# Moving elementwise terms of a recurrent layer from VectorE to ScalarE, one chunk later, and a longer lead into the output projection

## The chip, the cores and the metric

The program runs on one core of one Trainium2 chip. Five engines of the core matter here: TensorE (PE in the profile, its weight loads PEld), VectorE (DVE), ScalarE (ACT), GpSimd (POOL) and SyncE (SP, which issues the weight transfers). The metric is device time in microseconds of one execution. The kernel before took 3607.97 us, the median of three runs (3603.24 to 3646.27). The change is judged by the same metric; lower is better.

## What is computed

Two blocks run over one sequence of 256 tokens of width 2048. The change touches only the last layer of the second block: a recurrent layer with 4096 inner channels, followed by its output projection.

```python
def causal_depthwise_conv(x, w, b):            # w: 4 taps
    ...
    for k in range(CONV_WIDTH):
        y = y + xp[:, k:k + S] * w[k]
...
def rglru(x, wa, ba, wx, bx, lam):
    r = sigmoid(x @ wa + ba); ig = sigmoid(x @ wx + bx)   # per block of 256 channels
    log_a = -LRU_C * r * softplus(-lam)
    a = exp(log_a)
    mult = sqrt(max(-expm1(2.0 * log_a), 0.0))
    h[t] = a[t] * h[t - 1] + mult[t] * ig[t] * x[t]
...
u, z = split(rmsnorm(x) @ w_in)
y = rglru(conv(u)) * silu(z)
x = x + rmsnorm(y @ w_out)
```

The kernel writes -expm1(2 log a) as (a * a + 1) * tanh(-log a): the names below follow that ("th" the tanh, "ex" a, "q" its square, "v" the product, "mx" the max with 0, "sr" the square root).

## The kernel before, in words

**Tiles.** Activations lie transposed: channels on the 128 partitions, the 256 tokens along the row. All weights stream through in chunks of 128 x 2048 numbers (1 MB). A chunk c is loaded into one of three RAW buffers, split by ScalarE into a rounded high part (WH, function `hi`, L901) and by VectorE into the rest (WL, function `lo`, L1353). For each of its 16 blocks of 128 x 128, TensorE issues three matmuls of 256 columns (L449 to L451), 48 for a chunk. Activations are split in high and low parts in the same way.

**Rings.** RAW, WH and WL hold three chunks each. SyncE issues the transfer of chunk c when `lo(c - 3)` is done. `hi(c)` waits for its transfer and for TensorE to finish chunk c - 3. `lo(c)` waits for `hi(c)`, and TensorE starts chunk c after `lo(c)`. `hi_to(c + 2)` and `lo_to(c + 2)` in the programs mean that each engine prepares the chunk two ahead of the step c it is at.

**The recurrent stage.** It has 8 groups g of 512 channels, 9 chunks each, called x0 to x8 here: x0 to x3 give the four tiles of u, x4 to x7 the four tiles of z, x8 holds the gate weights of the group. Every engine's program is written out by hand as a loop over g and x (`pe_lru`, `act_lru`, `dve_lru`), and an engine executes in that order; semaphores join them. The elementwise work on group g - 1 (`recur_act`, `recur_dve`) is spread over the steps x of group g.

VectorE before, at step x: `lo` of the chunk two ahead; its part of the recurrence of the last group; then for x0 to x3 `lru_u`: take the tile of this same chunk out of PSUM times the norm factor (`scaled`, L1526), first tap with bias (L1986), three more taps (L1990), high part (L1993) and low part (L1995) of the result for the gate matmul; for x4 to x7 take the z tile out of PSUM (L1526), and one step later multiply by its sigmoid (L2007). The recurrence on VectorE: L1950 input times input gate (at x1), L1956 and L1959 square and product for tiles 0, 1 (x4) and 2, 3 (x5), L1963 the max (x6), L1966 and the scans L1969 (x7), L1975, L1977, L1979 times z and the two halves of y (x8).

ScalarE before: `hi` two ahead; eight sigmoids of the gates from PSUM (L1293, at x0), four tanh (L1301) and four exp (L1306) at x2, one square root (L1310) at x6; sigmoids of z (L1331) at x4 to x7. Tanh is in the table of the sigmoid; exp and square root need their own, and each change of table is an ACT_TABLE_LOAD row.

**The output projection.** 16 output tiles, each from two chunks, one for each half of the 4096 inner channels. The last group of y is ready last, so the stage begins with first halves only: in `pe_oproj` the first halves of tiles 0 to 3 ran before the second half of tile 0, in PSUM banks i % 4. During these four half tiles ScalarE and VectorE do the whole recurrence of group 7 (first lines of `act_oproj` and `dve_oproj`), where the weight chunks are split only in between. Bank 4 is used by the sums of squares, banks 4 to 7 by the gates of the recurrent stage.

## Time and profile before

| | |
|---|---|
| median of the runs | 3607.97 us (3603.24 to 3646.27) |
| the profiled execution | 3592.77 us, span 3591.5 us |
| TensorE matmul busy | 3446.9 us (96%), 29276 instructions |
| VectorE busy | 2321.5 us (65%) |
| ScalarE busy | 1610.6 us (45%) |
| weight traffic | 643.39 MB read, 185 GB/s over the span |
| mean granted TensorE clock | 0.984 |

The profiled execution is one of several; it is 0.4% below the median of the three. In the chain that ended last, TensorE has 60% of the span, VectorE 9%, ScalarE 5%. The two shares of busy time of the helpers are averages over stages that differ; the rows further down are from the stages that the change touches. The recurrent stage runs from about 2830 us to 3265 us, the output projection after it until about 3460 us.

### The profile page before, as it was taken

What the parts mean: (1) busy time and instruction counts of PE and PEld (TensorE: products, weight loads), DVE (VectorE), ACT (ScalarE), POOL (GpSimd) and SP (SyncE); (2) the same over time, 40 slices, a digit from 0 to 9 for tenths busy, and PEclk for the clock granted to TensorE, in tenths of its full rate; (3) what the DMA queues carried; (4) which work ended last, traced back from release to release, by engine and by line L of the source; (5) the groups of instructions that cost most, each with busy time, mean ns of one, the idle gap of its engine ahead of it and who ended that gap; (6) DMA issues with size and microseconds to landing.
All of it is one profiled execution on the core that took longest, in us unless ns stands there. A gap on an engine that the chain in (4) does not pass through costs nothing.

```text
span 3591.5 us, 66328 instructions
## 1 busy us (share of the span) xinstructions
PE 3446.9 (96%) x29276; PEld 3405.5 (95%) x29276; DVE 2321.5 (65%) x3076; ACT 1610.6 (45%) x1690; POOL 250.3 (7%) x196
## 2 busy tenths in 40 slices
PE   8999999999999999999999999999999798988988
PEld 8899999999999999999999999999999798988987
DVE  5676679875555555545555578786455787886455
ACT  4444444455543333444434433333445455555454
POOL 0000000488700000000000000000000000000000
PEclk9999999999999999999999999999999899999999
DMA  6334455555565665655566455555544344444543
GB/s 235 141 130 165 165 220 182 184 204 218 213 229 209 210 212 211 212 193 195 206 217 218 162 190 197 190 188 203 197 176 150 126 174 162 167 165 163 191 152 129
DMA packets 123887, 668.65 MB, mean 186 GB/s; under 512 B 10512, under 2 KB 44048, under 8 KB 45648
## 3 DMA queue, kind: packets, MB, share of 16 engines
q1 hardware_dynamic: 86688, 622.65, 48.8%
q10 hardware_dynamic: 36912, 41.75, 3.4%
q8 instruction: 231, 3.78, 0.4%
q14 instruction: 56, 0.46, 0.0%
HBM read 643.39 MB, written 20.97 MB: 185 GB/s over the span
## 4 chain that ended last, share of the span: by engine, by line
PE 60%; DVE 9%; ACT 5%; issue 4%; ACTq 0%; DVEq 0%
PE PS L449 20%; PE PS L450 20%; PE PS L451 20%; DVE WL L1353 3%; ACT WH L901 3%; PE PS L741 1%; DVE UCS L1990 1%; DVE IG L1969 0%; DVE UQ L1956 0%; DVE ZBS L1526 0%; ACT IG L1301 0%; DVE ZBS L1975 0%; DVE UCS L1950 0%; DVE UCS L1966 0%; ACT L1331 0%
## 5 line engine op out<-in xcount | busy, mean ns | idle before, releaser
L1353 DVE TENSOR_TENSOR WL<-RAW,WH 128x2048 fp32r<-128x2048 f32 x589 | 1350.3, 2293 | 1022.6 <-ACT WH L901 1022.2
L449 PE MATMUL PS<-A,WH 128*128 128x256 f32 x5648 | 1605.4, 284 | 79.5 <-DVE WL L1353 35.8
L450 PE MATMUL PS<-A,WH 128*128 128x256 f32 x5648 | 1578.7, 280 | 0.0
L451 PE MATMUL PS<-A,WL 128*128 128x256 f32 x5648 | 1578.1, 279 | 0.0
L901 ACT ACTIVATE WH<-RAW 128x2048 fp32r<-128x2048 f32 x589 | 1125.0, 1913 | 871.1 <-PE PS L451 851.4
L449 PEld LDWEIGHTS PS<-A,WH 128*128 128x128 f32 x5648 | 1077.0, 191 | 104.4 <-issue 61.8
L450 PEld LDWEIGHTS PS<-A,WH 128*128 128x128 f32 x5648 | 1076.1, 191 | 3.9 <-issue 2.9
L451 PEld LDWEIGHTS PS<-A,WL 128*128 128x128 f32 x5648 | 1074.9, 190 | 0.0
L449 PE MATMUL PS<-CO,WH 128*128 128x256 f32 x2048 | 571.2, 279 | 0.2
L450 PE MATMUL PS<-CO,WH 128*128 128x256 f32 x2048 | 571.0, 279 | 0.0
L451 PE MATMUL PS<-CO,WL 128*128 128x256 f32 x2048 | 571.0, 279 | 0.0
L449 PEld LDWEIGHTS PS<-CO,WH 128*128 128x128 f32 x2048 | 389.4, 190 | 0.6 <-issue 0.6
L450 PEld LDWEIGHTS PS<-CO,WH 128*128 128x128 f32 x2048 | 384.4, 188 | 0.0
L451 PEld LDWEIGHTS PS<-CO,WL 128*128 128x128 f32 x2048 | 384.4, 188 | 0.0
L449 PE MATMUL PS<-Y,WH 128*128 128x256 f32 x1152 | 321.6, 279 | 15.2 <-DVE WL L1353 15.2
L450 PE MATMUL PS<-Y,WH 128*128 128x256 f32 x1152 | 320.7, 278 | 0.0
L451 PE MATMUL PS<-Y,WL 128*128 128x256 f32 x1152 | 320.4, 278 | 0.0
L1694 POOL TENSOR_SCALAR OB<-IOTA,I2T,GTT 128x128 f32<-128x128 f32 x192 | 250.1, 1314 | 722.4 <-ACT GTT L1128 673.2
L1110 ACT ACTIVATE GA<-TMP 128x256 f32<-128x256 f32 x128 | 53.5, 418 | 407.7 <-DVE TMP L1526 407.7
L449 PEld LDWEIGHTS PS<-Y,WH 128*128 128x128 f32 x1152 | 218.5, 190 | 17.1 <-issue 10.0
L450 PEld LDWEIGHTS PS<-Y,WH 128*128 128x128 f32 x1152 | 218.6, 190 | 0.0
L451 PEld LDWEIGHTS PS<-Y,WL 128*128 128x128 f32 x1152 | 218.6, 190 | 0.0
(255 smaller groups left out, 2670.0 us busy)
## 6 DMA issues: line engine op xcount, KB each, us to landing
RAW<-in_w_in SPq DMA_DIRECT2D x177, 1024.0 KB, 4.7
RAW<-in_peer_down SPq DMA_DIRECT2D x128, 1024.0 KB, 4.8
RAW<-in_peer_up SPq DMA_DIRECT2D x128, 1024.0 KB, 5.3
RAW<-in_w_out SPq DMA_DIRECT2D x80, 1024.0 KB, 4.7
RAW<-in_w_gate SPq DMA_DIRECT2D x32, 1024.0 KB, 4.8
RAW<-in_w_query SPq DMA_DIRECT2D x16, 1024.0 KB, 4.8
gates_away<-XT ACTq DMA_DIRECT2D x16, 1024.0 KB, 5.9
RAW<-in_pool_w SPq DMA_DIRECT2D x16, 1024.0 KB, 4.8
```

The lines of the kernel that those rows point to most:

```text
L449: e.matmul(ps, wh, x[:, k, 0, :], start=first, stop=False, skip_group_check=True)
L450: e.matmul(ps, wh, x[:, k, 1, :], start=False, stop=False, skip_group_check=True)
L451: return e.matmul(ps, wl, x[:, k, 0, :], start=False, stop=last, skip_group_check=True)
L741: ins = e.matmul(BANK[5 + q % 2][:, k * 128:k * 128 + 128], OA[:, q % 2, k, :], OB[:, q % 2, k, :], start=True, stop=True, skip_group_chec ...
L901: e.activation(WH[:, c % NSPL, :], RAW[:, c % NRAW, :], ACT.Copy).then_inc(s_hi, 1)
L1110: e.activation(GA[:, jj, :], TMP[:, n_gelu[p, jj] % 2, :], ACT.Gelu_apprx_tanh).then_inc(s_gelu, 1)
L1353: e.tensor_tensor(WL[:, c % NSPL, :], RAW[:, c % NRAW, :], WH[:, c % NSPL, :].bitcast(F32), ALU.subtract).then_inc(s_lo, 1)
L1694: return e.tensor_scalar(OB[:, q % 2, k, :], IOTA[:, :], I2T[:, tok:tok + 1], GTT[:, tok:tok + 1], ALU.is_equal, ALU.mult)
L1990: e.scalar_tensor_tensor(UC[:, i, :], UQ[:, 1 + k:1 + k + T], vec("conv_w_2", 32 * k + n), UC[:, i, :], ALU.mult, ALU.add).then_inc(L1.sem ...
```

## The change

- **VectorE and ScalarE take a tile one chunk later.** The tile of chunk x - 1 is taken out of PSUM at step x, and `lo` comes behind the recurrence rather than ahead of it. UQ has two buffers for this.
- **Five terms go from VectorE to ScalarE**: the first tap with the bias (Identity with scale and bias), the high part of the convolved tile (Copy), the square "q" of all four tiles at once, the max with 0 (Relu), the high part of y (Copy). The product "v" becomes one instruction over four tiles. "th" and "q" are kept in YQ, which lies over the part of Y that the group's y will fill later.
- **Order in ScalarE**: tanh and exp at x1, q at x2, Relu and square root at x3, where they were at x2 and x6; the part of a step that belongs to the previous group comes last in it.
- **Output projection of this layer**: seven first halves lead (LEAD), not four; banks are dealt in turn from (0, 1, 2, 3, 5, 6, 7) for it and for what follows up to the gate chunks. The recurrence of group 7 is spread over the first six steps (RECUR_END), with `hi` and `lo` of a chunk in each. The first layer keeps four and gets the new banks only.

```diff
+LEAD = [4, 7]
+O_END = [[C_O[l] + (LEAD[l] + i if i < LEAD[l] else 2 * i + 1) for i in range(16)] for l in range(2)]
...
+    YQ = put("YQ", [128, 32, 2, T])
     place["at"] = base
-    UQ = put("UQ", [128, 4 + T])
+    UQ = put("UQ", [128, 2, 4 + T])
...
+        turn = itertools.cycle((0, 1, 2, 3, 5, 6, 7))
         for i in range(16):
-            plan(("o", l, i), i % 4, s_sq, 16 * (3 + 4 * l) + i + 1)
+            plan(("o", l, i), next(turn), s_sq, 16 * (3 + 4 * l) + i + 1)
         for x in range(2):
             for q in range(4):
                 n_eva += 1
                 EVA[l, x, q] = n_eva
-                plan(("e", l, x, q), (5, 6, 7, 0)[q] if x else q, s_eva, n_eva)
+                plan(("e", l, x, q), next(turn), s_eva, n_eva)
         for c in range(C_G[l], C_G[l] + 16):
-            plan_dve(c, c % 4)
+            plan_dve(c, next(turn))
...
-        c0 = C_O[l]
+        c0, n = C_O[l], LEAD[l]
         for hf in range(2):
-            for i in range(4):
-                c = c0 + 4 * hf + i
+            for i in range(n):
+                c = c0 + n * hf + i
                 if hf == 0:
                     wait_bank(e, ("o", l, i))
+                    if l and i == 4:
+                        e.wait_ge(RA.sem, RA.at(("ig", 7)))
...
-        for i in range(4, 16):
+        for i in range(n, 16):
             wait_bank(e, ("o", l, i))
...
         c0, m = C_O[l], 3 + 4 * l
-        if l == 1:
-            hi_to(e, c0 + 2)
-            recur_act(e, 7, 0)
-            recur_act(e, 7, 2)
-            hi_to(e, c0 + 3)
-            recur_act(e, 7, 6)
-        for i in range(4):
-            hi_to(e, c0 + i + 2)
-            if i == 2:
+        for j in range(LEAD[l]):
+            hi_to(e, c0 + j + 2)
+            if l == 1 and j < len(RECUR_END):
+                for x in RECUR_END[j]:
+                    recur_act(e, 7, x)
+            if j == 3:
...
-        if x == 2:
-            e.wait_ge(RD.sem, RD.at(("ui", g)))
+        if x == 1:
+            e.wait_ge(RA.sem, RA.at(("ig", g)))
             e.wait_ge(s_sp8[1], 8)
             for i in range(4):
                 n = 4 * g + i
-                ins = e.activation(IG[:, i, :], RG[:, i, :], ACT.Tanh, scale=SP8[:, 1, n:n + 1])
+                ins = e.activation(YQ[:, n, 0, :], RG[:, i, :], ACT.Tanh, scale=SP8[:, 1, n:n + 1])
             ins.then_inc(RA.sem, RA.one(("th", g)))
-            e.wait_ge(RA.sem, RA.at(("th", g)))
             for i in range(4):
                 n = 4 * g + i
                 ins = e.activation(RG[:, i, :], RG[:, i, :], ACT.Exp, scale=SP8[:, 2, n:n + 1])
             ins.then_inc(RA.sem, RA.one(("ex", g)))
-        if x == 6:
-            e.wait_ge(RD.sem, RD.at(("mx", g)))
+        if x == 2:
+            e.wait_ge(RA.sem, RA.at(("ex", g)))
+            e.activation(YQ[:, 4 * g:4 * g + 4, 1, :], RG[:, :, :], ACT.Square).then_inc(
+                RA.sem, RA.one(("q", g)))
+        if x == 3:
+            e.wait_ge(RD.sem, RD.at(("v", g)))
+            e.activation(IG[:, :, :], IG[:, :, :], ACT.Relu).then_inc(RA.sem, RA.one(("mx", g)))
+            e.wait_ge(RA.sem, RA.at(("mx", g)))
             e.activation(IG[:, :, :], IG[:, :, :], ACT.Sqrt).then_inc(RA.sem, RA.one(("sr", g)))
+        if x == 7:
+            e.wait_ge(RD.sem, RD.at(("zy", g)))
+            e.activation(Y[:, 4 * g:4 * g + 4, 0, :], ZBS[:, g % 2], ACT.Copy).then_inc(RA.sem, RA.one(("hi", g)))
...
                 if g or x > 1:
                     hi_to(e, c + 2)
-                if g:
-                    recur_act(e, g - 1, x)
-                if 4 <= x < 8:
-                    i = x - 4
-                    e.wait_ge(s_ev, EV[c])
+                if 1 <= x < 5:
+                    n = 4 * g + x - 1
+                    e.wait_ge(s_ev, EV[c - 1])
+                    e.activation(UCS[:, g % 2, x - 1, :], UQ[:, n % 2, 4:4 + T], ACT.Identity,
+                                 bias=vec("conv_b_2", n), scale=vec("conv_w_2", 96 + n)).then_inc(
+                        LA.sem, LA.one(("c3", g, x - 1)))
+                if 5 <= x:
+                    i = x - 5
+                    e.wait_ge(s_ev, EV[c - 1])
                     if 4 * g + i >= 2:
                         e.wait_ge(s_zm, 4 * g + i - 1)
                     e.activation(TMP[:, i % 2, :], ZBS[:, g % 2, i, :], ACT.Sigmoid).then_inc(s_zsig, 1)
+                if 2 <= x < 6:
+                    e.wait_ge(L1.sem, L1.at(("c0", g, x - 2)))
+                    e.activation(Y[:, 4 * g + x - 2, 0, :], UCS[:, g % 2, x - 2, :], ACT.Copy).then_inc(
+                        LA.sem, LA.one(("hi", g, x - 2)))
+                if g:
+                    recur_act(e, g - 1, x)
...
-        c0 = C_O[l]
+        c0, m = C_O[l], 3 + 4 * l
         if l == 1:
-            lo_to(e, c0 + 2)
-            recur_dve(e, 7, 1)
-            recur_dve(e, 7, 4)
-            recur_dve(e, 7, 5)
-            recur_dve(e, 7, 6)
-            lo_to(e, c0 + 3)
-            recur_dve(e, 7, 7)
-            recur_dve(e, 7, 8)
+            z_mult(e, 7, 3)
         for c in range(c0, C_E[l]):
...
+            if l == 1 and c - c0 < len(RECUR_END):
+                for x in RECUR_END[c - c0]:
+                    recur_dve(e, 7, x)
...
-        if x in (4, 5):
-            e.wait_ge(RA.sem, RA.at(("ex", g)))
-            for i in (2 * (x - 4), 2 * (x - 4) + 1):
-                if i:
-                    e.wait_ge(S.sem, S.at((f"v{i - 1}", g)))
-                e.tensor_tensor(UQ[:, 4:4 + T], RG[:, i, :], RG[:, i, :], ALU.mult).then_inc(
-                    S.sem, S.one((f"q{i}", g)))
-                e.wait_ge(S.sem, S.at((f"q{i}", g)))
-                e.scalar_tensor_tensor(IG[:, i, :], UQ[:, 4:4 + T], 1.0, IG[:, i, :], ALU.add, ALU.mult).then_inc(
-                    S.sem, S.one((f"v{i}", g)))
-        if x == 6:
-            e.wait_ge(S.sem, S.at(("v3", g)))
-            e.tensor_scalar(IG[:, :, :], IG[:, :, :], 0.0, None, ALU.max).then_inc(S.sem, S.one(("mx", g)))
-        if x == 7:
+        if x == 3:
+            e.wait_ge(RA.sem, RA.at(("q", g)))
+            e.wait_ge(S.sem, S.at(("ui", g)))
+            e.scalar_tensor_tensor(IG[:, :, :], YQ[:, 4 * g:4 * g + 4, 1, :], 1.0, YQ[:, 4 * g:4 * g + 4, 0, :],
+                                   ALU.add, ALU.mult).then_inc(S.sem, S.one(("v", g)))
+        if x == 5:
             e.wait_ge(RA.sem, RA.at(("sr", g)))
             e.tensor_tensor(UC, UC, IG[:, :, :], ALU.mult).then_inc(S.sem, S.one(("us", g)))
             e.wait_ge(S.sem, S.at(("us", g)))
-            for i in range(4):
+            for i in range(2):
+                e.tensor_tensor_scan(IG[:, i, :], RG[:, i, :], UC[:, i, :], 0.0, ALU.mult, ALU.add)
+        if x == 6:
+            for i in range(2, 4):
                 ins = e.tensor_tensor_scan(IG[:, i, :], RG[:, i, :], UC[:, i, :], 0.0, ALU.mult, ALU.add)
             ins.then_inc(S.sem, S.one(("sc", g)))
-        if x == 8:
-            n0 = 4 * g
             e.wait_ge(S.sem, S.at(("sc", g)))
             e.wait_ge(s_zm, 4 * g + 4)
             e.tensor_tensor(ZB, ZB, IG[:, :, :], ALU.mult).then_inc(S.sem, S.one(("zy", g)))
-            e.wait_ge(S.sem, S.at(("zy", g)))
-            e.tensor_copy(Y[:, n0:n0 + 4, 0, :], ZB).then_inc(S.sem, S.one(("hi", g)))
-            e.wait_ge(S.sem, S.at(("hi", g)))
-            e.tensor_tensor(Y[:, n0:n0 + 4, 1, :], ZB, Y[:, n0:n0 + 4, 0, :].bitcast(F32), ALU.subtract).then_inc(
-                S.sem, S.one(("lo", g)))
-
...
+    def lru_conv(e, g, i):
+
+        n = 4 * g + i
+        UC, U = UCS[:, g % 2, i, :], UQ[:, n % 2, :]
         for k in (2, 1, 0):
+            if k == 2:
+                e.wait_ge(LA.sem, LA.at(("c3", g, i)))
+            else:
+                e.wait_ge(L1.sem, L1.at((f"c{k + 1}", g, i)))
+            e.scalar_tensor_tensor(UC, U[:, 1 + k:1 + k + T], vec("conv_w_2", 32 * k + n), UC, ALU.mult,
+                                   ALU.add).then_inc(L1.sem, L1.one((f"c{k}", g, i)))
+
+    def lru_low(e, g, i):
+
+        n = 4 * g + i
+        e.wait_ge(LA.sem, LA.at(("hi", g, i)))
+        e.tensor_tensor(Y[:, n, 1, :], UCS[:, g % 2, i, :], Y[:, n, 0, :].bitcast(F32), ALU.subtract).then_inc(
             L1.sem, L1.one(("lo", g, i)))
+
+    def z_mult(e, g, i):
+        e.wait_ge(s_zsig, 4 * g + i + 1)
+        ZB = ZBS[:, g % 2, i, :]
+        e.tensor_tensor(ZB, ZB, TMP[:, i % 2, :], ALU.mult).then_inc(s_zm, 1)
 
     def dve_lru(e):
         c0 = C_L[1]
         for g in range(8):
             for x in range(9):
                 c = c0 + 9 * g + x
+                if 1 <= x < 5:
+                    scaled(e, c - 1, UQ[:, (4 * g + x - 1) % 2, 4:4 + T], 6)
+                if 5 <= x:
+                    scaled(e, c - 1, ZBS[:, g % 2, x - 5, :], 6)
+                if 2 <= x < 6:
+                    lru_low(e, g, x - 2)
+                if 6 <= x:
+                    z_mult(e, g, x - 6)
+                if g:
+                    if x == 0:
+                        z_mult(e, g - 1, 3)
+                    recur_dve(e, g - 1, x)
                 if g or x > 1:
                     lo_to(e, c + 2)
-                if g:
-                    recur_dve(e, g - 1, x)
-                if x < 4:
-                    lru_u(e, g, x, c)
-                if 4 <= x < 8:
-                    scaled(e, c, ZB[:, x - 4, :], 6)
-                if x > 4:
-                    z_mult(x - 5)
+                if 1 <= x < 5:
+                    lru_conv(e, g, x - 1)
```

ScalarE, a group in the middle of the recurrent stage, from the table load of exp to the square root, before (RG, IG: the gates; TMP<-ZBS: sigmoid of z; WH<-RAW: a weight split):

```order
L1306 ACT_TABLE_LOAD
L1306 ACTIVATE RG<-RG,SP_60 128x256 [waits recur_act]
L1306 ACTIVATE RG<-RG,SP_60 128x256 x3
L901 ACTIVATE WH<-RAW 128x2048 [waits chunk_used,raw_landed1]
L901 ACTIVATE WH<-RAW 128x2048 [waits chunk_used,raw_landed2]
L1331 ACT_TABLE_LOAD [waits z_multiplied]
L1331 ACTIVATE TMP<-ZBS 128x256 [waits evacuated_dve]
L901 ACTIVATE WH<-RAW 128x2048 [waits chunk_used,raw_landed0]
L1331 ACTIVATE TMP<-ZBS 128x256 [waits z_multiplied,evacuated_dve]
L901 ACTIVATE WH<-RAW 128x2048 [waits chunk_used,raw_landed1]
L1310 ACT_TABLE_LOAD
L1310 ACTIVATE IG<-IG 128x1024 [waits recur_dve]
```

and now (YQ<-RG: the square; UCS<-UQ and Y<-UCS: the two moved terms of the convolution):

```order
L1315 ACT_TABLE_LOAD
L1315 ACTIVATE RG<-RG,SP_60 128x256 x4
L914 ACTIVATE WH<-RAW 128x2048 [waits chunk_used,raw_landed0]
L1345 ACTIVATE UCS<-UQ,VEC 128x256 [waits evacuated_dve]
L1356 ACTIVATE Y<-UCS 128x256 [waits lru_dve]
L1319 ACTIVATE YQ<-RG 128x4x256 [waits recur_act]
L914 ACTIVATE WH<-RAW 128x2048 [waits chunk_used,raw_landed1]
L1345 ACTIVATE UCS<-UQ,VEC 128x256 [waits evacuated_dve]
L1356 ACTIVATE Y<-UCS 128x256 [waits lru_dve]
L1323 ACTIVATE IG<-IG 128x1024 [waits recur_dve]
L1325 ACT_TABLE_LOAD
L1325 ACTIVATE IG<-IG 128x1024 [waits recur_act]
```

The square root stood behind four splits and stands behind two, now with the Relu and its wait for VectorE (recur_dve) ahead of its table load; the tanh and exp as a whole come one split earlier, and the tanh waits for ScalarE's own sigmoids rather than for VectorE.

VectorE at the steps x1 to x3 of a group, before:

```order
L1353 TENSOR_TENSOR WL<-RAW,WH 128x2048 [waits chunk_high_made]
L1950 TENSOR_TENSOR UCS<-UCS,IG 128x1024 [waits recur_act]
L1526 TENSOR_TENSOR UQ<-PS,R 128x256 [waits r_made,chunk_used]
L1986 TENSOR_SCALAR UCS<-UQ,VEC 128x256 [waits evacuated_dve]
L1990 SCALAR_TENSOR_TENSOR UCS<-UQ,VEC,UCS 128x256 [waits lru_dve] x3
L1993 CAST Y<-UCS 128x256 [waits lru_dve]
L1995 TENSOR_TENSOR Y<-UCS,Y 128x256 [waits lru_dve]
L1353 TENSOR_TENSOR WL<-RAW,WH 128x2048 [waits chunk_high_made]
```

and now:

```order
L1973 TENSOR_TENSOR UCS<-UCS,IG 128x1024 [waits recur_act]
L1381 TENSOR_TENSOR WL<-RAW,WH 128x2048 [waits chunk_high_made]
L2006 SCALAR_TENSOR_TENSOR UCS<-UQ,VEC,UCS 128x256 [waits lru_act]
L2006 SCALAR_TENSOR_TENSOR UCS<-UQ,VEC,UCS 128x256 [waits lru_dve] x2
L1554 TENSOR_TENSOR UQ<-PS,R 128x256 [waits r_made,chunk_used]
L2013 TENSOR_TENSOR Y<-UCS,Y 128x256 [waits lru_act]
L1381 TENSOR_TENSOR WL<-RAW,WH 128x2048 [waits chunk_high_made]
```

The split WL<-RAW,WH stands ahead of the taps of its step now, and each low part (Y<-UCS,Y) waits for a copy by ScalarE (lru_act) and stands ahead of the next split.

VectorE at the start of the output projection, the recurrence of group 7, before:

```order
L1963 TENSOR_SCALAR IG<-IG 128x1024 [waits recur_dve]
L1353 TENSOR_TENSOR WL<-RAW,WH 128x2048 [waits chunk_high_made]
L1966 TENSOR_TENSOR UCS<-UCS,IG 128x1024 [waits recur_act]
L1969 SCALAR_TENSOR_TENSOR IG<-RG,UCS 128x256 [waits recur_dve]
L1969 SCALAR_TENSOR_TENSOR IG<-RG,UCS 128x256 x3
L1975 TENSOR_TENSOR ZBS<-ZBS,IG 128x1024 [waits z_multiplied,recur_dve]
L1977 CAST Y<-ZBS 128x4x256 [waits recur_dve]
L1979 TENSOR_TENSOR Y<-ZBS,Y 128x4x256 [waits recur_dve]
L1353 TENSOR_TENSOR WL<-RAW,WH 128x2048 [waits chunk_high_made] x2
```

and now:

```order
L1381 TENSOR_TENSOR WL<-RAW,WH 128x2048 [waits chunk_high_made]
L1977 SCALAR_TENSOR_TENSOR IG<-YQ 128x1024 [waits recur_dve,recur_act]
L1381 TENSOR_TENSOR WL<-RAW,WH 128x2048 [waits chunk_high_made]
L1981 TENSOR_TENSOR UCS<-UCS,IG 128x1024 [waits recur_act]
L1984 SCALAR_TENSOR_TENSOR IG<-RG,UCS 128x256 [waits recur_dve]
L1984 SCALAR_TENSOR_TENSOR IG<-RG,UCS 128x256
L1987 SCALAR_TENSOR_TENSOR IG<-RG,UCS 128x256 x2
L1991 TENSOR_TENSOR ZBS<-ZBS,IG 128x1024 [waits z_multiplied,recur_dve]
L1894 TENSOR_TENSOR P<-PT,P 128x2x256 [waits p_high_made]
L1381 TENSOR_TENSOR WL<-RAW,WH 128x2048 [waits chunk_high_made] x2
L1994 TENSOR_TENSOR Y<-ZBS,Y 128x4x256 [waits recur_act]
```

Before, one split stood between the max and the last low part of y, and the next ones behind it; now one stands on either side of the product "v" (IG<-YQ) and two more ahead of the last low part (Y<-ZBS,Y).

## Rows read from the trace of the kernel before

**Rows 1.** Busy time of each engine in six stretches, with matmul counts
```profile
core 0: us, PE busy (x) PEld busy (x) DVE busy (x) ACT busy (x) POOL busy (x), PEclk, DMA share, GB/s
2400.00:2600.00 200.00, 200.00 (x1765) 199.84 (x1765) 123.98 (x147) 78.19 (x65) 0.00 (x0) 1.00 0.55 196
...
2870.00:2920.00 50.00, 50.00 (x427) 50.00 (x426) 37.85 (x54) 28.56 (x32) 0.00 (x0) 1.00 0.49 171
...
2841.00:2865.00 24.00, 24.00 (x192) 24.00 (x193) 17.37 (x24) 6.95 (x7) 0.00 (x0) 0.93 0.61 215
2865.10:3257.30 392.20, 364.27 (x3026) 359.59 (x3024) 313.90 (x431) 210.35 (x234) 0.00 (x0) 0.98 0.47 167
3257.30:3307.90 50.60, 39.24 (x290) 38.50 (x290) 37.00 (x40) 26.50 (x31) 0.00 (x0) 0.90 0.42 151
```

**Rows 2.** TensorE timeline: start, duration, first matmul of six chunks, idle before
```profile
3084.91 0.38 PE L449 MATMUL PS<-Y,WH 128*128 128x256 f32 x1 [0.84 <-DVE WL L1353]
...
3092.57 0.36 PE L449 MATMUL PS<-A,WH 128*128 128x256 f32 x1 [1.93 <-DVE WL L1353]
...
3101.07 0.36 PE L449 MATMUL PS<-A,WH 128*128 128x256 f32 x1 [1.08 <-DVE WL L1353]
...
3118.54 0.36 PE L449 MATMUL PS<-A,WH 128*128 128x256 f32 x1 [0.67 <-DVE WL L1353]
...
3135.84 0.36 PE L449 MATMUL PS<-A,WH 128*128 128x256 f32 x1 [0.72 <-DVE WL L1353]
...
3142.38 0.38 PE L449 MATMUL PS<-Y,WH 128*128 128x256 f32 x1 [0.84 <-DVE WL L1353]
```

**Rows 3.** ScalarE timeline of the same group
```profile
3113.09 1.71 ACT L1301 ACTIVATE IG<-RG,SP 128x256 f32<-128x256 f32 x4 [4.10 <-DVE UCS L1950]
3114.82 1.28 ACT L1306 ACT_TABLE_LOAD   x1
3116.12 1.71 ACT L1306 ACTIVATE RG<-RG,SP 128x256 f32<-128x256 f32 x4
...
3142.96 1.06 ACT L1310 ACTIVATE IG<-IG 128x1024 f32<-128x1024 f32 x1 [1.66 <-DVE IG L1963]
3144.04 1.28 ACT L1331 ACT_TABLE_LOAD   x1
...
3145.66 1.90 ACT L901 ACTIVATE WH<-RAW 128x2048 fp32r<-128x2048 f32 x1
```

**Rows 4.** VectorE timeline of the same group
```profile
3107.41 1.52 DVE L1990 SCALAR_TENSOR_TENSOR UCS<-UQ,VEC,UCS 128x256 f32<-128x256 f32 x3
...
3142.24 0.69 DVE L1963 TENSOR_SCALAR IG<-IG 128x1024 f32<-128x1024 f32 x1
...
3147.59 2.29 DVE L1353 TENSOR_TENSOR WL<-RAW,WH 128x2048 fp32r<-128x2048 f32 x1 [4.00 <-ACT WH L901]
3149.80 1.22 DVE L1966 TENSOR_TENSOR UCS<-UCS,IG 128x1024 f32<-128x1024 f32 x1
3151.06 2.44 DVE L1969 TENSOR_TENSOR_SCAN IG<-RG,UCS 128x256 f32<-128x256 f32 x4
```

**Rows 5.** VectorE groups by shape, first 300 us: busy, mean ns
```profile
L1400 DVE SCALAR_TENSOR_TENSOR XT<-XT 128x1024 f32<-128x1024 f32 x1 | 1.2, 1220 | 0.0
```

**Rows 6.** TensorE timeline: the waits of 2840 us and of 3257 to 3308 us
```profile
2840.91 0.55 PE L449 MATMUL PS<-A,WH 128*128 128x256 f32 x1 [2.94 <-DVE WL L1353]
...
3265.11 0.36 PE L449 MATMUL PS<-Y,WH 128*128 128x256 f32 x1 [1.88 <-DVE WL L1353]
...
3273.48 0.36 PE L449 MATMUL PS<-Y,WH 128*128 128x256 f32 x1 [2.47 <-DVE WL L1353]
...
3291.71 0.55 PE L449 MATMUL PS<-Y,WH 128*128 128x256 f32 x1 [5.17 <-DVE WL L1353]
...
3300.68 0.39 PE L449 MATMUL PS<-Y,WH 128*128 128x256 f32 x1 [1.84 <-DVE WL L1353]
```

**Rows 7.** Page, DMA issues: KB each, us from issue to landing
```profile
RAW<-in_w_in SPq DMA_DIRECT2D x177, 1024.0 KB, 4.7
```

55 lines of the change are left out of this document (22 added, 33 removed).

## The prediction, made before the changed kernel ran

> **What bounds the kernel now.** I read the busy time by stretches first, to see where TensorE falls short of its own pace. In a stretch where it never waits it issues 1765 matmuls in 200 us, 113.3 ns each, so a chunk of 48 takes 5.44 us and a group of nine 49.0; there is a slightly slower unbroken pace too, 427 in 50 us, 117.1 ns, 5.62 a chunk, and the granted clock is 1.00 in both [rows 1]. From the gate chunk of group 0 to that of group 7 lie 392.2 us for seven groups of 432 matmuls: 3024 x 113.3 ns is 342.7, so 49.5 us are lost there. In the next 50.6 us 290 matmuls need 32.9, so 17.7 are lost at the start of the output projection [rows 1]. That is the whole prize, with a few us at the start of the stage: about 72.
>
> The TensorE timeline says who is late. A group repeats after 3142.38 - 3084.91 = 57.47 us, and TensorE waits in it at five places, 0.67 to 1.93 us each, every time for VectorE's part of a weight split, L1353 [rows 2]. The two longest are those of x0 and x1. VectorE is busy 313.9 of 392.2 us, ScalarE 210.4 [rows 1]; neither is full, so the delay is in the order. Ahead of the split that x0 waits for, VectorE idles 4.00 us for ScalarE, and ScalarE sits in a row of square root, table load and z sigmoid before its own part of the split at 3145.66; the square root had waited 1.66 for VectorE's max [rows 3, 4]. So each engine's recurrence terms hold up the other's weight split. At the start of the output projection the waits are 1.84 to 5.17 us; there most of the recurrence of group 7 stands between two splits [rows 6].
>
> **The prices.** From the rows: ScalarE split 1.90, VectorE split 2.29, four tanh or four exp 1.71, table load 1.28, square root over 1024 columns 1.06, three taps 1.52, a product over 1024 columns 1.22, four scans 2.44, the max 0.69 [rows 3, 4]. An operation that waits for nothing starts 0.08 before the end of the last (3147.59 + 2.29 against 3149.80), one on the other engine 0.03 after its cause [rows 3, 4]. So in a row I count split 1.83 and 2.22, taps 1.56 with their own waits, a scan 0.58, and 0.11 for each change of engine. The new operations have no row. "v" over 1024 columns: the same instruction in another stage took 1.220 [rows 5], which I take; below it can't go by much, above it lie the four single ones at about 0.45, 1.8. Relu, square and copy over 1024: as the square root, 1.06. The tap on ScalarE: as one of the four tanh, 0.41 in a row and some 0.5 alone (3 x 0.41 + 0.5 is 1.7); its copy 0.36, about the time between the end of the load (3145.32) and the split at 3145.66, where one z sigmoid runs [rows 3]; I take 0.41 and 0.36.
>
> **Part 1, the recurrent stage.** T = 0 is when TensorE starts x0. Its end at 5.44 is signalled at 5.73. *ScalarE*: split of x3 1.83, tap 0.41, tanh 1.70, load 1.28, exp 1.70, split of x4 1.83, tap 0.41, copy 0.36: 15.25. (The eight sigmoids before it end in time: split from 0.3 and 8 x 0.43 make 5.6.) *VectorE*: change 0.11, low part 0.40, split of x4 2.22, taps 1.56, next tile out of PSUM 0.36: 19.90. *ScalarE* tap and copy with the change 0.88, *VectorE* low part 0.51 and v 1.22: 22.51. *ScalarE* Relu 1.20, load 1.28, root 1.00, split of x6 1.83, tap and copy 0.77: 28.59. *VectorE* low part 0.51, split of x6 2.22, taps 1.56, tile x4 out 0.36: 33.24. *ScalarE* sigmoid and copy 0.83; *VectorE* low part 0.51, product 1.22, two scans 1.16, split of x7 2.22, and 0.21 until TensorE starts: 39.39. At 5.44 a chunk TensorE could start x7 at 38.10. It is 1.3 us late, once a group; the splits of x4 (17.98 against 21.8), x5, x6 and x8 come in time. A group takes 49.0 + 1.3 = 50.3; at the slower pace x7 is wanted at 39.3 and a group takes 50.6 to 50.9. The same bookkeeping on the order of before gives 57.7 against 57.47, with waits at the same places, so I trust it to about 0.5. I take 50.5: 392.2 - 7 x 50.5 = **38.7 us**. The moved work (about 6 us a group) leaves VectorE near 39 of 50 and puts ScalarE near 36.
>
> One load of four a group goes: the root's neighbours no longer split the z sigmoids. Each load costs 1.28 and the next operation begins 0.02 after it (3114.82 + 1.28 against 3116.12) [rows 3]. The Trainium skill ("ScalarE: Activation LUTs", What ACT_TABLE_LOAD costs) counts about 1.38 us of drain besides the 1.28, 2.66 a switch; by it the two loads on the chain would add 2.8 and a group would take 53. The trace shows no such second part.
>
> Relu on ScalarE costs more than the max it replaces, 1.06 against 0.69, and it costs a cover: an engine that waits has its load behind it already (before, the load for the root ended while ScalarE waited for the max [rows 3]), now the load comes after the Relu. With the max on VectorE the root would be ready some 1.8 us sooner and the 1.3 us of x7 would vanish. The skill's rule (the same page, Rules for kernel authors) is to use VectorE for relu and max; by it this one move is wrong by up to 9 us over seven groups, by my sum too.
>
> Transfers: each starts when VectorE's split three chunks earlier is done. The tightest is x2 of the next group: issued at 44.5, wanted at 50.6, and it lands in 4.7 [rows 7]. It holds with 1.4 us to spare. Should it go, TensorE has another 5 us of split chunks ahead.
>
> **Part 2, output projection.** By the same prices after the end of x8: gates 5.1, split to 7.6, tanh, load and exp 12.2, split 14.1, square 15.1; VectorE's split to 16.4 and v 17.6; Relu, load, root 21.1; splits to 25.3; product, four scans, product with z 30.1; low part of p 30.7; split of the seventh chunk 33.0, for which TensorE asks at 32.7 (0.5 late with the start); the last low part of y 36.5, asked for at 7.75 x 5.44 = 42.2. So seven half tiles cover it, with 5.7 us in hand; without that cover it would cost what it does now. The four waits (1.88, 2.47, 5.17, 1.84 [rows 6]) and the lowered clock that comes with them (0.90 over 50.6 us [rows 1]) go: 17.7 - 0.5 = **17.2 us**.
>
> **Part 3, the first chunks.** TensorE waits 2.94 us at 2840.91 for the split of x4, which stands behind two whole tiles of convolution [rows 6]. Now one tile's taps and one low part stand there: 2.2 us sooner, and the lowered clock after the wait (0.93 over 24 us [rows 1], worth 1.7) may go: **3.5 us**.
>
> **Part 4, nothing.** Banks in turn: no row shows TensorE waiting for a bank, the waits are all for L1353. Four half tiles of the first layer stay.
>
> **Sum.** 38.7 + 17.2 + 3.5 = 59.4, less 1 for a chance that the freed stretch runs at the slower pace (3.7% on the 150 us behind, at about one in five): 58.5. The profiled execution, 3592.77, would become 3534; against the median, 3607.97, which lies 15 above it, 3549.5, a saving of 1.6%.
>
> **Rivals.**
> 1. *The chain on ScalarE is longer than I count* (0.20). If each of the two loads on it held the engine for a load's time more, 2 x 1.28, a group would take 52.9 and the stage would give 392.2 - 370 = 22; in all 42: **3566**. By the skill's price of a switch it is the same case. Taps at 0.50, changes of engine 0.04 slower and splits at full length add 1.6 and lie between. Against it: the rows 3 on the loads.
> 2. *No wait is left* (0.12): the 1.3 us at x7 are within my error. All of 72 less a little: **3537**.
> 3. *The gain is given back* (0.05): what is earlier in the projection waits at its end or the stage runs at the slower pace throughout. For it, 117.1 ns in the first group of the stage [rows 1]; it takes 10 to 15 us: **3563**. A transfer that is late counts here: at 1 MB in 5.44 us, 193 GB/s, while 196 were moved in a stretch without a wait [rows 1].
> 4. *Slower* (0.03): every high part of a chunk stands behind a wait for VectorE now, and every low part behind one for ScalarE, so a delay on either goes round. The chain from 5.73 to 39.18 is 33.5 us; its excess lengthens the group one for one. It decides when a group passes 57.5 + 20.7/7 = 60.4, 10 us more than I count, each of its ten changes of engine costing 1.1 instead of 0.11; 2% slower needs 18 more: **3680**. The 0.03 of the rows speak against it.
>
> The rest, 0.60, is the forecast, by itself 3540 to 3560. Two per cent, 72 us, is about what a measurement of this kernel can tell from no change; the runs before span 43. Faster by more than that takes all of the prize, or most and a low median: 0.11. Slower by more: 0.02. The range goes from rival 2 less 12 for the spread of medians, 3525, to rival 1 plus 14, 3580.
>
> **What would show it.** A group of 50 to 51 us with one wait left, before x7; no lowered clock inside the stage; no wait over 1 us in the seven leading half tiles; three table loads a group on ScalarE. Wrong if waits stand before x4 or x6 (the low part's wait for ScalarE dearer), or if the last low part of y comes after the seventh half tile.

## The result

The changed kernel took 3559.6 us (median of four runs, 3550.42 to 3580.24), the kernel before, beside it, 3618.31 (four runs, 3603.24 to 3646.27): a ratio of 0.9875, with a 95% interval of 0.984 to 0.991. That is 1.25% less time, clear of no change but under two per cent. The median is 10 us above the 3549.5 predicted and inside the range. How much was saved depends on what is compared. The two medians lie 58.7 us apart, the ratio makes it 45 (33 to 58), and the two profiled executions, 3557.89 us against 3592.77, differ by 34.9. The sum had said 58.5. Stages can be compared only in the profiled pair, so what follows is mostly about the 23.6 us that are missing there.

The page of the changed kernel, its busy row and its chain:

```profile
PE 3455.3 (97%) x29276; PEld 3418.6 (96%) x29276; DVE 2268.5 (64%) x2940; ACT 1654.3 (47%) x1771; POOL 249.5 (7%) x196
...
PE 71%; DVE 3%; ACT 2%; issue 2%; DVEq 0%; ACTq 0%
```

The waits left the chain (VectorE 9% to 3%, ScalarE 5% to 2%). TensorE has the same 29276 matmuls and yet 8 us more of busy time than before, which is the first sign of what happened. By stretches (busy us with counts for each engine, granted clock, DMA share, GB/s), those of [rows 1] at their new places:

```profile
2845.43:2876.98 31.55, 30.44 (x244) 30.09 (x243) 23.57 (x31) 17.91 (x20) 0.00 (x0) 0.94 0.47 166
2876.98:3233.14 356.16, 356.16 (x3027) 356.16 (x3026) 273.50 (x321) 250.19 (x308) 0.00 (x0) 1.00 0.52 184
3233.14:3283.74 50.60, 50.60 (x432) 50.60 (x431) 33.11 (x24) 31.21 (x34) 0.00 (x0) 1.00 0.58 207
3233.14:3419.70 186.56, 186.56 (x1587) 186.56 (x1586) 92.83 (x62) 86.75 (x88) 0.00 (x0) 1.00 0.54 192
```

From the gate chunk of group 0 to that of group 7 TensorE never waits, at a granted clock of 1.00; the same holds for the first 50.6 us of the projection, 432 matmuls where [rows 1] had 290. But 432 in 50.6 us is 117 ns each, not 113.3. The stage gave 392.2 - 356.16 = 36.0. From the gate chunk of group 7 to the first matmul on p (the operand of the stage that follows the projection) it was 197.41 before and is 186.56: 10.9. The row of before, which ends later than the one in [rows 1]:

```profile
3257.32:3454.73 197.41, 186.05 (x1586) 185.33 (x1585) 103.64 (x81) 87.86 (x88) 0.00 (x0) 0.97 0.51 182
```

The start of the stage gave 35.04 - 31.55 = 3.5. The sum of these is 50.4; that the pair differs by less is because the program up to the stage, which the change does not touch, took 2845.43 us instead of 2830.06.

TensorE's timeline shows the last wait before the stage and the next after it; between them lie 577 us without one (start, duration, first matmul, idle before it in brackets):

```profile
2854.29 0.36 PE L460 MATMUL PS<-A,WH 128*128 128x256 f32 x1 [1.11 <-DVE WL L1381]
...
3432.31 0.36 PE L460 MATMUL PS<-A,WH 128*128 128x256 f32 x1 [0.84 <-DVE WL L1381]
```

ScalarE in one group (x0 starts at 3086.15), beside [rows 3]: the tap on ScalarE, the copy, the square, the Relu with the load behind it. ScalarE has three table loads a group now, as forecast (24 in the stage and behind it, 31 before):

```profile
3100.80 0.58 ACT L1345 ACTIVATE UCS<-UQ,VEC 128x256 f32<-128x256 f32 x1
3101.29 0.40 ACT L1356 ACTIVATE Y<-UCS 128x256 fp32r<-128x256 f32 x1
3101.60 1.05 ACT L1319 ACTIVATE YQ<-RG 128x1024 f32<-128x1024 f32 x1
...
3108.70 1.06 ACT L1323 ACTIVATE IG<-IG 128x1024 f32<-128x1024 f32 x1 [1.63 <-DVE IG L1977]
3109.78 1.28 ACT L1325 ACT_TABLE_LOAD   x1
3111.07 1.07 ACT L1325 ACTIVATE IG<-IG 128x1024 f32<-128x1024 f32 x1
```

VectorE in the same group, beside [rows 4]:

```profile
3101.73 0.42 DVE L2013 TENSOR_TENSOR Y<-UCS,Y 128x256 fp32r<-128x256 f32 x1 [3.64 <-ACT Y L1356]
3102.07 2.28 DVE L1381 TENSOR_TENSOR WL<-RAW,WH 128x2048 fp32r<-128x2048 f32 x1
...
3107.11 0.42 DVE L2013 TENSOR_TENSOR Y<-UCS,Y 128x256 fp32r<-128x256 f32 x1 [0.98 <-ACT Y L1356]
3107.45 1.22 DVE L1977 SCALAR_TENSOR_TENSOR IG<-YQ 128x1024 f32<-128x1024 f32 x1
...
3122.75 2.27 DVE L1381 TENSOR_TENSOR WL<-RAW,WH 128x2048 fp32r<-128x2048 f32 x1
```

The last row is the split of x7. It ends at 3125.02, 38.87 after x0's start; I had worked out 39.18. TensorE at 117.8 ns a matmul (5.65 us a chunk) wants x7 at 39.57, so nothing waits. The first row is VectorE idling 3.64 us for the small copy that the change moved to ScalarE; the last experiment comes back to it.

### The profile page after: what moved, and what is told of

It is laid out like the page before. It is cut to its first block, busy times and chain, and to the rows that moved or that the text cites. A ratio compares the mean times of both kernels' runs of the same rounds, so it can differ in the third digit from the quotient of the medians.

```text
span 3556.6 us, 66273 instructions
## 1 busy us (share of the span) xinstructions
PE 3455.3 (97%) x29276; PEld 3418.6 (96%) x29276; DVE 2268.5 (64%) x2940; ACT 1654.3 (47%) x1771; POOL 249.5 (7%) x196
## 4 chain that ended last, share of the span: by engine, by line
PE 71%; DVE 3%; ACT 2%; issue 2%; DVEq 0%; ACTq 0%
PE PS L460 23%; PE PS L461 23%; PE PS L462 23%; ACT WH L914 1%; PE PS L752 1%; DVE WL L1381 1%; DVE XT L1955 0%; DVE A L1392 0%; DVE EE L1952 0%; ACT SQ L928 0%; DVE XT L1777 0%; PE PS L494 0%; DVE TMP L1554 0%; DVE OO L1405 0%; DVE EE L1929 0%
```

## TensorE has two paces, and most of the gap is there

In a stretch without a wait TensorE issues a matmul either every 113.3 ns or every 117.8, at a granted clock of 1.00 in both, and it stays with one for hundreds of us. The same two stretches of 200 us, in a stage that the change does not touch, in the kernel before, in the changed one, and in the changed one run once more:

```profile
1060.00:1260.00 200.00, 200.00 (x1701) 200.00 (x1700) 104.35 (x106) 79.54 (x72) 0.00 (x0) 1.00 0.60 210
1780.00:1980.00 200.00, 200.00 (x1767) 200.00 (x1766) 109.15 (x111) 81.08 (x73) 0.00 (x0) 1.00 0.60 214
```

```profile
1060.00:1260.00 200.00, 200.00 (x1767) 200.00 (x1766) 108.35 (x112) 82.14 (x74) 0.00 (x0) 1.00 0.63 216
...
1780.00:1980.00 200.00, 200.00 (x1701) 200.00 (x1700) 103.86 (x106) 79.87 (x72) 0.00 (x0) 1.00 0.62 209
```

```profile
1060.00:1260.00 200.00, 200.00 (x1767) 200.00 (x1766) 108.35 (x110) 82.16 (x74) 0.00 (x0) 1.00 0.63 216
1780.00:1980.00 200.00, 200.00 (x1700) 200.00 (x1700) 104.52 (x106) 79.31 (x72) 0.00 (x0) 1.00 0.62 210
```

Either stretch can have 1767 or 1701. I counted, from the starts of the matmuls in each trace, those at the slower pace up to the norm before the stage (the same code in all of these kernels) and set them against the time at which TensorE gets there:

```
execution              matmuls at 117.8 ns   us up to the norm
before                        4939               2830.06
changed                       8291               2845.43
e2_lead7_only                 7647               2845.88
e6_chain3                    10500               2854.53
e12_changed_again            11625               2858.59
e1_lead4                     14671               2872.44
e3_relu_dve                  15394               2874.44
```

The line through the first and the last is 4.2 ns a matmul; the two paces differ by 4.4 to 4.5. What is left over goes with the time that TensorE spent at the lowered clock, which differs too: 57.5 us of it up to the norm before, 51.2 in e3_relu_dve, and 64.3 in e2_lead7_only, which lies some 4 us above the line. So the 15.4 us that the unchanged part lost in the changed kernel's profile is nearly all pace. The executions that were not profiled show no pace, but it is likely to be much of why those of one kernel differ by 19 to 48 us: with the pace held (below) the spread falls to 9 to 13. The experiments asked first whether the change did what the sum says once the pace is set aside, and then what sets the pace.

## Experiments

**Each part of the change alone.** `e1_lead4` keeps the new stage and goes back to four leading half tiles:

```diff
-LEAD = [4, 7]
+LEAD = [4, 4]
-    RECUR_END = [(0,), (1,), (2, 3), (5, 6), (7,), (8,)]
+    RECUR_END = [(0,), (1,), (2, 3), (5, 6, 7, 8)]
```

> The changed kernel with the recurrent stage as it is and four leading half tiles instead of seven; the recurrence of group 7 stands behind the splits of the first four chunks of the projection. By my prices the last low part of y is done some 32 to 33 us after the end of group 7's gate chunk and TensorE asks for it at 4.75 x 5.44 = 25.8 (26.8 at 5.65 a chunk): one wait of 6 to 7 us there and a lowered clock after it, so the stretch from the gate chunk of group 7 to the first matmul on p is 7 to 9 us longer than with seven (186.56). The seven groups of the stage stay as they are after the change (50.1 to 50.9 each). Rival, that the order of the recurrence alone gave what the projection gained: 0 to 2 us longer.

Ratio to before 0.9862 (0.9817 to 0.9907). The wait for y is there, of the size expected:

```profile
3298.38 0.58 PE L460 MATMUL PS<-Y,WH 128*128 128x256 f32 x1 [5.56 <-DVE Y L1994]
...
3260.15:3448.76 188.61, 183.05 (x1586) 182.85 (x1585) 93.14 (x62) 86.83 (x88) 0.00 (x0) 0.98 0.53 190
```

But the stretch is only 2.0 us longer than with seven (188.61 against 186.56), not 7 to 9. The wait broke a stream at the slower pace, and it went on at the faster one: 1287 of the 1585 matmuls, at some 4.4 ns each, gave about 5.6 us back. A wait of 5.6 us, with a lowered clock behind it (0.98), cost 2.

`e2_lead7_only` is the kernel before with the lead alone, and group 7's recurrence spread behind the splits of the first five chunks:

```diff
+LEAD = [4, 7]
...
-            recur_act(e, 7, 0)
-            recur_act(e, 7, 2)
-            hi_to(e, c0 + 3)
-            recur_act(e, 7, 6)
+        for j in range(LEAD[l]):
+            hi_to(e, c0 + j + 2)
+            if l == 1 and j < 3:
+                recur_act(e, 7, (0, 2, 6)[j])
...
+            if l == 1:
+                for x in {0: (1,), 1: (4, 5, 6), 3: (7,), 4: (8,)}.get(c - c0, ()):
+                    recur_dve(e, 7, x)
```

> The kernel before with only the second part of the change: seven leading half tiles, banks in turn, the recurrence of group 7 spread over the first five splits, all its operations on the engines of before. The stage stays at 392 (389 to 395) for seven groups. From the gate chunk of group 7 to the first matmul on p 197.4 becomes 180 to 186 (all of the 17.7 that are lost there at 5.44 us a chunk, less 0 to 6 for the slower pace), with no wait over 1 us for the splits. Rival, that the projection needs the stage's shorter chain: y comes after 42 us and a wait of 2 to 6 us stands at the last quarter of the second half tile.

Ratio 0.997 (0.9937 to 1.0002). The stage stayed (391.74), the projection went to 192.76, a miss. 1381 of its matmuls ran at the slower pace (6.0 us), and three waits of the old kind are left:

```profile
3279.66 0.36 PE L455 MATMUL PS<-Y,WH 128*128 128x256 f32 x1 [1.84 <-DVE WL L1357]
...
3288.06 0.36 PE L455 MATMUL PS<-Y,WH 128*128 128x256 f32 x1 [1.09 <-DVE WL L1357]
...
3306.29 0.36 PE L455 MATMUL PS<-Y,WH 128*128 128x256 f32 x1 [1.44 <-DVE WL L1357]
```

The wait of 5.17 of [rows 6] is gone, those before the first chunks are not: the helpers still carry the stage's old recurrence. So the lead alone brought 4.7 us of the projection's 10.9, and 0.3% of the whole, which its interval does not tell from nothing. The new stage alone, e1_lead4, brought 8.8 there, and its total (3561.32) is not told from that of the whole change (3559.6).

**The Relu's engine.** `e3_relu_dve` puts the Relu back on VectorE as a max, right behind v:

```diff
-            e.activation(IG[:, :, :], IG[:, :, :], ACT.Relu).then_inc(RA.sem, RA.one(("mx", g)))
-            e.wait_ge(RA.sem, RA.at(("mx", g)))
...
+            e.wait_ge(S.sem, S.at(("v", g)))
+            e.tensor_scalar(IG[:, :, :], IG[:, :, :], 0.0, None, ALU.max).then_inc(S.sem, S.one(("mx", g)))
```

> The changed kernel with the Relu of the recurrence back on VectorE as a max. VectorE's split of x7 should end about 1.8 us sooner after x0's start (38.86 in the changed kernel, so 37.0 to 37.5). Theory A (TensorE has two steady paces, 113.4 and 117.8 ns a matmul, drawn anew only when its stream is interrupted; the changed kernel's stage ran without a wait at the slower one): no wait in the seven groups and one pace throughout them, so 356.2 us at the slower pace (no difference to the changed kernel) or 343 at the faster, about one chance in two each. Theory B (the chain through the Relu on ScalarE is what bounds the group at 50.88): every group comes to 49.0 to 49.5, whatever the pace before it.

Ratio 0.9898 (0.9851 to 0.9945), seven groups 356.15: nothing gained at the slower pace, as theory A has it. The size of the step on the chain was wrong: the split of x7 ended 38.43 after x0, 0.43 sooner and not 1.8. The root did start earlier, its load now under the wait, but VectorE's next low part waits as long as before for ScalarE's copy of a convolution tile:

```profile
3085.21 1.28 ACT L1323 ACT_TABLE_LOAD   x1
3087.55 1.06 ACT L1323 ACTIVATE IG<-IG 128x1024 f32<-128x1024 f32 x1 [1.06 <-DVE IG L1978]
...
3092.03 0.40 ACT L1354 ACTIVATE Y<-UCS 128x256 fp32r<-128x256 f32 x1
```

```profile
3092.47 0.42 DVE L2013 TENSOR_TENSOR Y<-UCS,Y 128x256 fp32r<-128x256 f32 x1 [0.98 <-ACT Y L1354]
```

**Is the chain the one I summed?** `e6_chain3` lengthens it (one execution, as for the two runs after it):

```diff
             e.wait_ge(RA.sem, RA.at(("mx", g)))
+            for k in range(3):
+                e.activation(YQ[:, 4 * g:4 * g + 4, 1, :], IG[:, :, :], ACT.Square).then_inc(
+                    RA.sem, RA.one((f"w{k}", g)))
+                e.wait_ge(RA.sem, RA.at((f"w{k}", g)))
             e.activation(IG[:, :, :], IG[:, :, :], ACT.Sqrt)
```

> The changed kernel with three more squares over 1024 columns on ScalarE between the Relu and the root, each behind the one before (added work, written where nobody reads any more). That is some 3.3 us on the chain that my sum goes by. Theory A (the chain from x0's end to VectorE's split of x7 is as I counted it; its end has 0.5 to 0.7 us to spare at the slower pace of TensorE, and 1.3 too little at the faster by my sum): the split of x7 ends at about 42.2 after x0's start, TensorE waits 2.5 to 3.5 us before x7 in every group, and a group comes to 53.1 to 53.6. The wait draws the pace anew each time, so both paces are seen in the stage. Theory B (another engine or a transfer bounds the group): the group grows by clearly less than 2.3 us.

The split of x7 ended at 42.14, and the first four groups took 53.07 to 53.48. TensorE's waits in one of them, before x6 and before x7:

```profile
3033.12 0.35 PE L460 MATMUL PS<-A,WH 128*128 128x256 f32 x1 [0.59 <-DVE WL L1385]
...
3040.73 0.36 PE L460 MATMUL PS<-A,WH 128*128 128x256 f32 x1 [1.73 <-DVE WL L1385]
```

So 3.3 us on the chain came out one for one behind the slack, though at two places where I had expected one. The last three groups took 54.7 to 55.2, which I had not expected: there the granted clock fell to 0.5 for 3.4 us in each, behind these waits, and cost another 1.7. And now that every group had waits, both paces appeared (1512 matmuls at the slower, 1298 at the faster).

**What draws the pace.** `e5_pulses` puts one extra matmul, never read, ahead of each chunk of the stage, in a kernel with the max on VectorE:

```diff
+                    n = PULSE[(x + 3 * g) % 8]
+                    e.matmul(BANK[bank[c]][:, T:T + n], WH[:, c % NSPL, 0:128], A[:, 0, 0, 0:n], start=True,
+                             stop=True, skip_group_check=True)
```

> The kernel with the max on VectorE, and ahead of each w_in chunk of the recurrent stage one more matmul into columns of the bank that nobody reads, of 16, 32, 48, 64, 96, 128, 192 or 256 columns in turn (it adds work, 0.05 to 0.15 us each, some 6 us in all). It asks whether an irregular step of TensorE's stream alone, without a wait, draws the pace anew. Theory A: the pace of 16-block chunks changes at these matmuls, each way, and both paces appear in the stage, perhaps always the same one after the same length. Theory B (the pace hangs on what the other engines or transfers do): the pace is the same on both sides of most of these matmuls and changes elsewhere, or stays at the slower pace throughout.

The pace changed at these matmuls and in no other place of the stage. One of 64 columns, from the trace; the starts lie 0.11 apart before it and 0.12 after it, with no wait anywhere:

```profile
2991.86 0.28 PE L461 MATMUL PS<-A,WH 128*128 128x256 f32 x1
2991.97 0.28 PE L462 MATMUL PS<-A,WL 128*128 128x256 f32 x1
2992.08 0.19 PE L893 MATMUL PS<-A,WH 128*128 128x64 f32 x1
2992.11 0.36 PE L460 MATMUL PS<-A,WH 128*128 128x256 f32 x1
2992.31 0.28 PE L461 MATMUL PS<-A,WH 128*128 128x256 f32 x1
2992.43 0.28 PE L462 MATMUL PS<-A,WL 128*128 128x256 f32 x1
```

All 17 of at most 96 columns that met the faster pace were followed by the slower one. `e8_survey` did the same ahead of every whole chunk of the program, with ten lengths in random order.

> The kernel with the max on VectorE and ahead of every whole chunk of 48 matmuls, in all stages of the program, one more matmul with the same stationary tile into columns of the bank that nobody reads, its length drawn from 16, 64, 128, 144, 160, 176, 192, 208, 224 and 240 columns (added work, about 0.11 us each, some 350 of them). In the runs before, lengths up to 96 always led from the faster pace to the slower and 192 left the faster one as it was. Theory A (the pace is a relation in time between TensorE's own instructions): the same length from the same pace leads to the same pace nearly always in every stage; there may be a length that leads from the slower pace to the faster and never back. Theory B: the pace after such a matmul is a coin flip whatever its length.

Counted from its trace, and leaving out those next to a wait or a lowered clock:

```
columns   from faster: stays / to slower    from slower: to faster / stays
  16            0 / 6                             3 / 13
  64            0 / 5                             5 / 6
 128            0 / 14                           15 / 6
 144            0 / 5                             5 / 6
 160            0 / 14                            4 / 14
 176            0 / 13                            9 / 15
 192            9 / 0                            11 / 9
 208           14 / 0                             6 / 14
 224            8 / 0                             5 / 8
 240            0 / 15                            9 / 6
```

From the faster pace the length decides without exception, 103 cases. The lengths 192, 208 and 224 keep it, the seven others lose it. From the slower one any length may lead out, in 3 of 16 cases (16 columns) to 15 of 21 (128). So a matmul of 192 columns is a one-way door: it can lead to the faster pace and did not lead away from it.

**The door used.** `e9_lock` (max on VectorE), `e10_lock_changed` (the changed kernel) and `e11_lock_before` (the kernel before) get 81 to 84 such matmuls, at the heads of the long stretches and twice a group in the stage:

```diff
+    def pulse(e, ps, c, b, x, k):
+        e.matmul(ps, WH[:, c % NSPL, b * 128:b * 128 + 128], x[:, k, 0, 0:192], start=True, stop=True,
+                 skip_group_check=True)
...
         e.wait_ge(s_lo, c + 1)
+        if c in LOCK:
+            pulse(e, BANK[bank[c]][:, T:T + 192], c, 0, x, 0)
         for b in range(16):
```

> The kernel with the max on VectorE, and a matmul of 192 columns into columns that nobody reads (added work, about 0.11 us each, some 85 of them) at the head of every long unbroken stretch of TensorE and one or two times a group in the recurrent stage. In the survey a matmul of 192 columns left the faster pace as it was in all of 9 cases and led from the slower to the faster in 11 of 20. Theory A (the pace is such a relation in time): nearly all long stretches run at 113.4 ns; the program up to the end of the norm before the stage takes 2820 to 2835 us (2830 to 2874 in the runs so far), seven groups 343 to 346 without a wait, from the gate chunk of group 7 to p 180 to 182, the whole some 3522 (3512 to 3540), and the runs spread less. Theory B (the pace is set by the chip or by transfers, and the survey's pattern was chance): both paces in the long stretches as before, 3555 to 3590.

> The changed kernel itself (Relu on ScalarE) with the same added matmuls of 192 columns. At the faster pace its chain should end too late for x7: the split of x7 ended 38.86 after x0's start at the slower pace, so 38.65 at the faster, where x7 is wanted at 38.08. Theory A: a wait of 0.6 to 0.8 us before x7 in each group, which draws the pace anew for x7 and x8, so a group takes 49.7 to 50.1 and seven 348 to 351; the whole some 5 us above the kernel with the max on VectorE, 3518 to 3545. It tells what the change would have brought at the faster pace that my sum was made with: 392.2 less about 349.5, 43 in the stage against the 38.7 forecast.

> The kernel before with the same added matmuls of 192 columns. Theory A: the part up to the stage 2820 to 2835 us as in the changed kernel with them, the stage 388 to 393 for seven groups (its waits hold it, whatever the pace), from the gate chunk of group 7 to p 190 to 198, the whole 3575 to 3595. The difference to the changed kernel with them is then the worth of the change without the lottery of the pace: 55 to 63 us, against the 58.5 of my sum. Theory B: no difference to the kernel before.

> The changed kernel once more, unchanged, on the chip of these runs, to see which paces its profiled execution shows this time. Theory A: up to the stage between 2830 and 2875 us by the number of matmuls at the slower pace at 4.35 ns each, the stage at 50.88 a group if it enters it at the slower pace as in the three runs before, and a median of 3550 to 3570. Theory B: the same paces at the same places as in the first profile.

All four ran beside the same runs of before:

| | median us | range | ratio to before (95%) |
|---|---|---|---|
| e9_lock | 3519.39 | 3515.25 to 3524.29 | 0.9756 (0.9718 to 0.9794) |
| e10_lock_changed | 3518.66 | 3515.08 to 3523.87 | 0.9755 (0.9718 to 0.9793) |
| e11_lock_before | 3582.17 | 3576.17 to 3589.04 | 0.9913 (0.9883 to 0.9944) |
| e12_changed_again | 3567.95 | 3559.71 to 3578.51 | 0.9889 (0.9849 to 0.9929) |

49 us come off the changed kernel by adding 84 useless matmuls, and its spread falls from 19 to 9 us. Of the kernel before 26 us come off, and its spread falls from 47.6 to 12.9. The stretches of e10_lock_changed (up to the norm; seven groups; gate chunk of group 7 to p) and its wait in a group:

```profile
0.00:2815.24 2815.24, 2742.38 (x23612) 2710.02 (x23613) 1795.26 (x2423) 1225.35 (x1240) 249.60 (x196) 0.99 0.55 194
2846.40:3197.29 350.89, 347.81 (x3040) 346.63 (x3039) 272.80 (x320) 247.69 (x306) 0.00 (x0) 1.00 0.52 187
3197.29:3377.60 180.31, 180.31 (x1593) 180.31 (x1592) 93.60 (x63) 87.44 (x89) 0.00 (x0) 1.00 0.56 199
...
2990.96 0.36 PE L460 MATMUL PS<-A,WH 128*128 128x256 f32 x1 [0.44 <-DVE WL L1396]
```

and the last two of e11_lock_before:

```profile
2857.06:3249.05 391.99, 362.58 (x3041) 357.57 (x3039) 315.06 (x431) 210.93 (x235) 0.00 (x0) 0.98 0.48 169
3249.05:3444.86 195.81, 184.74 (x1589) 184.03 (x1590) 103.62 (x81) 87.86 (x88) 0.00 (x0) 0.97 0.51 183
```

The waits of e10_lock_changed show how the pace is drawn: it has one of 0.43 to 0.46 us before x7 in each of the seven groups, and behind five of them TensorE went on at the slower pace, behind two at the faster.

Misses: e9_lock was not faster than e10_lock_changed. Its seven groups took 348.65, only 2.2 less than those of e10_lock_changed and not 343 to 346, because VectorE's split of x8 ended 43.6 to 43.9 after x0 and x8 was wanted at 43.5, 43.7 with the two added matmuls. And the difference to e11_lock_before is 63.5 us, just above the 55 to 63 expected. The changed kernel run once more did not repeat its first paces upstream (11625 matmuls at the slower one, 8291 the first time), as theory A has it, but entered the stage at the slower one again:

```profile
2890.13:3246.29 356.16, 356.16 (x3026) 356.16 (x3025) 273.52 (x321) 250.15 (x308) 0.00 (x0) 1.00 0.52 184
```

**Is it the length, or any extra matmul?** `e13_160_columns` is e10_lock_changed with 160 for 192:

```diff
-        e.matmul(ps, WH[:, c % NSPL, b * 128:b * 128 + 128], x[:, k, 0, 0:192], start=True, stop=True,
+        e.matmul(ps, WH[:, c % NSPL, b * 128:b * 128 + 128], x[:, k, 0, 0:160], start=True, stop=True,
```

> The changed kernel with the same added matmuls at the same places as in the run with 192 columns, but 160 columns long, which is 32 columns less work each. In the survey 160 columns led from the faster pace to the slower in 14 of 14 cases, and from the slower to the faster in 4 of 18. Theory A (what these matmuls do is set the pace, by their length): nearly all long stretches run at 117.8 ns; up to the norm before the stage 2865 to 2895 us against 2815 with 192 columns, seven groups 357 to 359 without a wait, 187 from there to p, the whole 3580 to 3605, slower than the changed kernel. Theory B (any extra matmul there helps, or the gain came from somewhere else): within 10 us of the 3519 with 192 columns.

3588.49 us, ratio 0.9924 (0.9891 to 0.9958), where 192 columns had 3518.66 and 0.9755: 70 us slower by the medians, 61 by the ratios, for less work. It needed 2894.60 us up to the norm. Only the stage fell outside what I had said, 353.88 us with both paces.

**One moved term undone.** `e14_copy_on_vector` is e10_lock_changed with the high part of the convolution tiles back on VectorE:

```diff
-                    e.activation(Y[:, 4 * g + x - 2, 0, :], UCS[:, g % 2, x - 2, :], ACT.Copy).then_inc(
-                        LA.sem, LA.one(("hi", g, x - 2)))
...
+        e.tensor_copy(Y[:, n, 0, :], UCS[:, g % 2, i, :]).then_inc(L1.sem, L1.one(("hi", g, i)))
```

> The changed kernel with the added matmuls of 192 columns, and one of the five moved terms undone: the high part of each convolution tile (256 columns, four a group) is made on VectorE again, right ahead of the low part. VectorE pays about 0.40 a tile, ScalarE gives back 0.36, and one change of engine (0.11) a tile goes. Theory A (the gain is in the order, a tile one chunk later, and not in each moved term): the split of x7 ends within 0.5 of the 38.76 of the kernel with the copies on ScalarE and a group takes 49.8 to 50.5. Theory B (VectorE is so full that each term moved off it counts): the split of x7 ends 0.8 to 1.6 later, a group 50.9 to 51.7, the whole 6 to 11 us longer.

Neither theory: the split of x7 came 3.56 us sooner, at 35.20, and no wait is left at the faster pace. A group takes 49.19. VectorE from 18.3 us after x0, and the seven groups:

```profile
3027.35 0.42 DVE L1565 TENSOR_TENSOR UQ<-PS,R 128x256 f32<-128x256 f32 x1
3027.69 0.28 DVE L2024 CAST Y<-UCS 128x256 fp32r<-128x256 f32 x1
3028.01 0.43 DVE L2026 TENSOR_TENSOR Y<-UCS,Y 128x256 fp32r<-128x256 f32 x1
3028.35 1.22 DVE L1988 SCALAR_TENSOR_TENSOR IG<-YQ 128x1024 f32<-128x1024 f32 x1
...
2856.02:3200.33 344.31, 344.31 (x3040) 344.31 (x3039) 283.27 (x349) 243.60 (x280) 0.00 (x0) 1.00 0.54 192
```

The copy costs VectorE 0.28, and the low part follows it at once, where it had idled 3.64, 0.98 and 2.13 us for ScalarE's. Of the first of these 2.20 stays, now ahead of the split behind it, for which VectorE waits on ScalarE's part. 6.6 us of the stage are gained (350.89 to 344.31), 0.9 a group: the rest of the 3.56 is slack that nobody waited for. The median, 3518.72 (0.9725, 0.9665 to 0.9784), does not tell it from e10_lock_changed: its profiled execution had lost 10.4 us upstream again, where the clock was lowered for 64.3 us in all against 39.6. e9_lock, e10_lock_changed and e14_copy_on_vector all beat both kernels; none of the three is told from the others by time.

## Why the prediction came out as it did

The total was right within its range, and so was most of the mechanism. The 10 us between 3549.5 and the measured 3559.6 are the base: the sum was taken off 3607.97, the median of three executions, and the median of four is 3618.31. That the two medians then lie 58.7 apart, against 58.5 forecast, is in good part luck, for executions of one kernel spread over 30 to 43 us in that comparison, the ratio makes it 45, and the changed kernel run once more lay 40 below the kernel before beside it. The stages of the profiled pair show what was right and what was not.

**Part 1, the chain.** The mechanism held. The split of x7 ended 38.87 after x0's start (39.18 forecast), that of x4 at 18.2 (17.98), and the lengthened chain moved the group one for one. A group took 50.88, where 50.5 was forecast: 36.0 for seven instead of 38.7. The wait before x7 that I had put at 1.3 us is 0.4 at the faster pace (with two added matmuls ahead of it, which alone put x7 off by 0.2), and none at the slower. Rival 1 falls: behind the load at 3109.78 + 1.28 the root starts 0.01 later, at 3111.07, and a group takes 50.88, not 53; the drain that the Trainium skill counts besides the load ("ScalarE: Activation LUTs", What ACT_TABLE_LOAD costs) is not seen here either.

**Part 2, the projection.** 10.9 instead of 17.2 in the profile, but no wait in it. The last low part of y was done 36.5 us after the end of x8, as forecast, and an estimated 7 us ahead of the need (7.75 chunks of 5.65). With the pace held the same stretch went from 195.81 to 180.31, 15.5. e1_lead4 and e2_lead7_only share out most of it: the lead takes away the wait for y (5.56), the shorter stage the waits for splits (4.4 together). Neither run shares out the rest; e11_lock_before had 10.2 us at the lowered clock there, e10_lock_changed none, which at half speed is worth an estimated 5.1.

**Part 3** gave the 3.5 forecast, by the terms forecast: the wait fell from 2.94 to 1.11 us and the lowered clock from 7.4 to 3.6. (The two terms of the prediction, 2.2 and 1.7, make 3.9, not 3.5.) **Part 4**: no wait for a bank is seen.

**The term that was mis-sized** is the one behind the sum: "less 1 for a chance that the freed stretch runs at the slower pace (3.7% on the 150 us behind, at about one in five)". All of the 4898 matmuls between the two waits ran at the slower pace. The projection lost 6.3 of its 17.2 by it. The stage fell only 2.7 short, because the slower pace also spares it the wait before x7. And for the part upstream, which the change does not touch, the sum had no term at all, as if both executions would draw the same paces there: it took 15.4 more. 2.7 + 6.3 - 1 + 15.4 is 23.4 of the 23.6 us missing. I had the two paces on the page [rows 1] (117.1 against 113.3 is 3.4%, the full stretches give 3.9) and priced them as a small risk of one stretch. Rival 3 named the slower pace throughout the stage at 0.05, with 3563, nearer to the 3559.6 measured than the forecast was. Its condition held in all four executions that were profiled with the new stage and without added work (the changed kernel twice, e1_lead4, e3_relu_dve).

With e11_lock_before and e10_lock_changed most of the lottery is out: 41.1 in the stage, 15.5 behind it and 2.0 at its head make 58.6 (58.5 forecast). That this meets the forecast to 0.1 is luck too, with 2.4 more in the stage, 3.2 less in the other two and the 1 for the slower pace not spent. The medians differ by 63.5 us and the profiled executions by 66.0. In the latter pair 8.7 us more lie upstream, again in code that is the same: there the clock was lowered for 62.4 us with e11_lock_before and for 39.6 with e10_lock_changed, while the matmuls at the slower pace were nearly as many.

Why always the slower one? At the faster pace this stage has a wait before x7 in each group (e10_lock_changed), and each wait draws anew; at the slower one it has none, and the pace stays. Once drawn it is kept. That fits all the stages seen; no run showed the changed stage fall from the one into the other, since all began slow, so this much is argued. Why all four began slow, behind waits of 1.03 to 1.13 us at the head of the stage, is open.

**The Trainium skill's rule on relu** ("ScalarE: Activation LUTs", Rules for kernel authors: VectorE for relu and max). I had it worth up to 9 us by my own sum. The durations agree with it (1.06 against 0.69), but it was worth 0.43 us a group on the chain, 2.2 us in the stage of e9_lock, and nothing that the totals show (3519.39 against 3518.66). The term that did sit on the wrong engine was one I had taken as given: the 256-column copy, whose price I set at 0.36 against 0.40. Its place, behind taps on the other engine and an exp row on its own, held the chain up by 3.6 us a group; at the faster pace that was worth 0.9 us a group in time, and at the slower pace, at which the changed kernel ran, no wait was left for it to remove.

## What to carry to other kernels

Where two engines hand tiles to each other in a fixed order, price a moved operation by what it stands behind and who idles for it, not by its own duration: a copy of 0.28 us held the other engine's chain up by 3.6. Then ask what of that anybody waits for: it was 0.9. Before reading a difference of one or two per cent, count matmuls per us in an unbroken stretch that the change does not touch. And when a change removes a kernel's waits, ask at which pace the unbroken stream will then run.

## What the runs showed of the hardware

The two steady paces of a stream of weight load and 128x256 matmul, 113.3 and 117.8 ns at a granted clock of 1.00, go by a relation in time between TensorE's own instructions, as far as these runs can tell: one matmul of another length can switch them (from the faster pace in 72 of 72 cases for seven of the lengths, in none of 31 for three), with the programs of the other engines left as they were. A wait draws the pace anew (five slower, two faster in e10_lock_changed), and so can a stretch of lowered clock: in e6_chain3 a stream at 113.3 ns came out of the one at 3148 us at 117.8, with no wait between. A single start that is late by 10 to 20 ns can do it too (in the kernel before at 2934 us). Without any of these the pace stayed for as long as the stream lasted, 577 us in the changed kernel. The Trainium skill gives N / 2.4 + 2.5 ns for one matmul behind another ("TensorE: Matmul & The Clock Gate", Back-to-back issue gap), an estimated 109.2 for 256 columns, and says that in a real kernel the weight load takes part in the spacing; the trace has neither 109.2 nor one single figure. An extra matmul of 16 to 192 columns costs the same here, some 0.11 us, about one place in the stream. Why 192 to 224 columns keep the faster pace and 176 and 240 do not stays open.
